# Turning the loops of a q and k projection, and sending a row of 1/rms through DRAM

## The reference

```python
h = rmsnorm(x, g_mix[l])
proj = h @ w_in[l]
qa = split_heads(proj[..., 0:MOBA_WIDTH], MOBA_HEADS)
ka = split_heads(proj[..., MOBA_WIDTH:2 * MOBA_WIDTH], MOBA_HEADS)
va = split_heads(proj[..., 2 * MOBA_WIDTH:o1], MOBA_HEADS)
qb = split_heads(proj[..., o1:o1 + SB_WIDTH], SB_HEADS)
kbh = split_heads(proj[..., o1 + SB_WIDTH:o1 + 2 * SB_WIDTH], SB_HEADS)
...
x = x + cross_attention(rmsnorm(x, g_cross[l]), rmsnorm(mem, g_mem[l]), w_xq[l], w_xkv[l], w_xo[l])
```

## Time and profile before

| | us |
|---|---|
| median of 3 runs | 451.23 |
| lowest, highest | 449.95, 452.59 |
| span of the profiled execution | 449.3 |
| PE busy in it | 438.3 (98%) |
| PEld busy | 400.4 (89%) |
| DVE busy | 271.3 (60%) |
| ACT busy | 213.4 (47%) |
| POOL busy | 25.1 (6%) |

### The profile page before, as it was taken

The page is one execution under the profiler, slowest core; times in us unless marked ns, Lnnn a source line. Parts: engine busy times, 40 slices in busy tenths (PEclk is TensorE's granted clock), DMA queues, the critical chain, the costliest instruction groups (busy, mean ns, idle before and its releaser), DMA issues.

```text
span 449.3 us, 6925 instructions
## 1 busy us (share of the span) xinstructions
PE 438.3 (98%) x2884; PEld 400.4 (89%) x2884; DVE 271.3 (60%) x340; ACT 213.4 (47%) x268; POOL 25.1 (6%) x39
## 2 busy tenths in 40 slices
PE   6999999999999999999999999999999999999993
PEld 6999988989998999988998889999999999999982
DVE  4769556866666534886567867655555555555525
ACT  5753338755545471382527654444444444444413
POOL 0079000000000000000020000000000000000001
PEclk9899999999999999999999999999999999999999
DMA  7998554333322235455443335555555555556002
GB/s 228 415 420 342 188 187 171 112 103 128 136 104 95 94 137 179 171 206 202 144 182 140 116 119 188 188 188 187 188 187 188 189 187 187 187 187 233 0 0 93
DMA packets 12970, 77.46 MB, mean 172 GB/s; under 512 B 1552, under 2 KB 2064, under 8 KB 4496
## 3 DMA queue, kind: packets, MB, share of 16 engines
q1 hardware_dynamic: 12800, 77.08, 46.9%
q10 hardware_dynamic: 144, 0.02, 0.0%
HBM read 76.04 MB, written 1.05 MB: 172 GB/s over the span
## 4 chain that ended last, share of the span: by engine, by line
PE 95%; DVE 1%; DMA 1%; ACT 1%; SPq 0%; issue 0%; POOLq 0%; POOL 0%; DVEq 0%; ACTq 0%
PE bank L856 41%; PE bank L875 33%; PE bank L971 11%; PE bank L1007 2%; DMA xT_raw<-in_xT_dram 1%; PE bank L1053 1%; PE bank L1008 1%; PE bank L929 1%; PE bank L1073 1%; PE bank L934 1%; PE bank L928 1%; PE bank L889 1%; DVE res L808 1%; PE bank L989 1%; PE bank L940 1%; DVE xs L814 0%
## 5 line engine op out<-in xcount | busy, mean ns | idle before, releaser
L554 DVE TENSOR_TENSOR w_lo<-raw,w_hi 128x2048 fp32r<-128x2048 f32 (+3 forms) x76 | 155.4, 2069 | 43.0 <-ACT w_hi L363 41.6
L363 ACT ACTIVATE w_hi<-raw 128x2048 fp32r<-128x2048 f32 x65 | 122.3, 1909 | 36.0 <-PE bank L856 19.4
L856 PE MATMUL bank<-hT_hi,w_hi 128*128 128x256 f32 x416 | 119.4, 287 | 2.9 <-DVE w_lo L554 2.4
L856 PE MATMUL bank<-hT_lo,w_hi 128*128 128x256 f32 x416 | 118.8, 286 | 0.0
L856 PE MATMUL bank<-hT_hi,w_lo 128*128 128x256 f32 x416 | 118.8, 286 | 0.0
L856 PEld LDWEIGHTS bank<-hT_hi,w_hi 128*128 128x128 f32 x416 | 81.0, 195 | 4.2 <-DVE hT_lo L576 2.6
L856 PEld LDWEIGHTS bank<-hT_lo,w_hi 128*128 128x128 f32 x416 | 81.0, 195 | 0.6
L856 PEld LDWEIGHTS bank<-hT_hi,w_lo 128*128 128x128 f32 x416 | 81.0, 195 | 0.0
L510 ACT ACTIVATE relu<-bank 128x512 f32<-128x512 f32 x16 | 9.6, 598 | 95.7 <-PE bank L856 95.7
L777 DVE TENSOR_TENSOR relu<-relu 128x512 f32<-128x512 f32 x16 | 11.1, 693 | 61.6 <-ACT relu L510 61.6
L875 PE MATMUL bank<-w_hi,aT_hi 128*128 128x512 f32 x144 | 46.0, 392 | 0.0
(11 more groups left out here) (156 smaller groups left out, 610.8 us busy)
## 6 DMA issues: line engine op xcount, KB each, us to landing
raw<-in_weights_dram SPq DMA_DIRECT2D x65, 1024.0 KB, 4.8
raw<-in_weights_dram SPq DMA_DIRECT2D x7, 256.0 KB, 6.3
raw<-in_weights_dram SPq DMA_DIRECT2D x2, 512.0 KB, 7.8
res<-in_x_dram SPq DMA_DIRECT2D x2, 512.0 KB, 11.9
mem_tok<-in_mem_dram SPq DMA_DIRECT2D x1, 1024.0 KB, 9.6
memT_raw<-in_memT_dram SPq DMA_DIRECT2D x1, 1024.0 KB, 8.3
out_dram<-xs SPq DMA_DIRECT2D x2, 512.0 KB, 2.6
xT_raw<-in_xT_dram SPq DMA_DIRECT2D x3, 256.0 KB, 5.5
```

The lines of the kernel that those rows point to most:

```text
L363: copy(w_hi[:, slot, :], raw[:, rslot, :], ACT.Copy).then_inc(w_hi_ready, 1)
L554: return nc.vector.tensor_tensor(dst, whole, high.bitcast(fp32), sub)
L856: last = mm(outs[m], w, v[:, k0 + k, :], start=first and n == 0, stop=k == nk - 1 and n == 2, skip_group_check=bool(kt_wait))
```

## The change

The first eight chunks are laid out anew: chunk k now holds the k-th 128 channels of all 2048 q and k columns. PE goes through k outermost; for each k it runs 16 column blocks m, three matmuls each, into all eight banks, which all stay open until k = 7. Chunks 0 to 2 come in pieces of whole column blocks: 2, 4 and 10 blocks for chunk 0, 8 and 8 for chunks 1 and 2. `xT` comes in eight transfers, one ahead of each k. The row of 1/rms goes to a scratch in DRAM in two transfers of 128 values, and comes back in two transfers that repeat it on all partitions, in SP's queue behind load 7 (for x) and load 14 (for the memory tokens). DVE takes all eight banks out one behind the other.

```diff
-    cols = [("w_in", 0, 8, base + 256 * j, 256) for base in (0, qkv) for j in range(4)]
+    cols = [("w_in", k, 1, (0, qkv), 1024) for k in range(8)]
...
-    X_PIECES = [(0, 1), (1, 2), (2, 4), (4, 6), (6, 8)]
-    PIECES = [(0, *p) for p in X_PIECES] + [(1, k, k + 2) for k in range(0, 8, 2)] + [(2, 0, 4), (2, 4, 8)]
+    QK = 16
+    PIECES = [(0, 0, 2), (0, 2, 6), (0, 6, 16), (1, 0, 8), (1, 8, 16), (2, 0, 8), (2, 8, 16)]
...
+            def row(j, n, ready, dst):
+                sp.wait_ge(rstd_ready, ready)
+                for t in range(TOK):
+                    sp.dma_start(rstd_dram[j, t * P:(t + 1) * P].rearrange("(p a) -> p a", a=1), rstd[:, n, t:t + 1])\
+                        .then_inc(rstd_out[j], 16)
+                sp.wait_ge(rstd_out[j], 32)
+                sp.dma_start(dst[:, 0, :], rstd_dram[j:j + 1, :].to_broadcast([P, SEQ])).then_inc(row_ready[j], 16)
+                sp.dma_start(dst[:, 1, :], rstd_dram[j:j + 1, :].to_broadcast([P, SEQ])).then_inc(row_ready[j], 16)
...
+                if c == 7:
+                    row(0, X, 1, rstd_row)
+                if c == 14:
+                    row(1, MEM, 2, mem_row)
...
-            dve.wait_ge(ident_ready, 1)
-            diagonal(X, 1)
-            split(4)
-            spread(rstd_row, X_ROW_BANK, 1)
-
-            dve.wait_ge(row_ready, 1)
+            split(8)
+            split(9)
+            dve.wait_ge(row_ready[0], 32)
             for c in range(8):
-                dve.wait_ge(w_used, c + 1)
+                dve.wait_ge(*((qk_done, c + 1) if c < 7 else (w_used, KT)))
                 nc.vector.scalar_tensor_tensor(flat(qkT[:, 2 * c:2 * c + 2, :]), bank[c][:, :],
                                                DH ** -0.5 if c % 4 < 2 else 1.0, flat(rstd_row[:, :, :]),
                                                ALU.mult, ALU.mult).then_inc(qk_evac, 1)
-                split(c + 5)
+            split(10)
+            split(11)
+            split(12)
...
-            for c in range(8):
-                if c == X_ROW_BANK:
-                    pe.wait_ge(row_ready, 1)
-                weights_T(c, hT_hi, hT_lo, 0, KT, halves(c), c + 1 if c > 2 else None,
-                          pieces_of(c) if c <= 2 else None,
-                          (lambda: spread_rstd(X_ROW_BANK, 1)) if c == 3 else None)
+            for k in range(KT):
+                pe.wait_ge(lo_done[X], k + 1)
+                if k > 2:
+                    pe.wait_ge(w_lo_ready, k + 1)
+                for m in range(QK):
+                    for i, (c, m0, m1) in enumerate(PIECES):
+                        if (c, m0) == (k, m):
+                            pe.wait_ge(*((w_lo_ready, c + 1) if m1 == QK else (piece_lo, piece_no(i))))
+                    wh, wl = w_hi[:, k % RING, m * P:m * P + P], w_lo[:, k % RAW, m * P:m * P + P]
+                    for n, (w, v) in enumerate(((wh, hT_hi), (wh, hT_lo), (wl, hT_hi))):
+                        last = mm(halves(m // 2)[m % 2], w, v[:, k, :], start=k == 0 and m % 2 == 0 and n == 0,
+                                  stop=k == KT - 1 and n == 2, skip_group_check=True)
+                    if k == KT - 1 and m % 2 and m + 1 < QK:
+                        last.then_inc(qk_done, 1)
+                last.then_inc(w_used, 1)
```

More of the change, by code:

```diff
@@ L244, in load_piece @@
             def load_piece(i):
[L245 to L257, removed]
+                c, m0, m1 = PIECES[i]
+                cols = slice(m0 * P, m1 * P)
+                sp.dma_start(raw[:, c, cols], weights[c, :, cols]).then_inc(raw_in[c] if m1 == QK else piece_in[i], 16)
+            def row(j, n, ready, dst):
[7 more added lines that the diff above has]
+            for k in range(KT):
+                sp.dma_start(xT_raw[:, k, :], xT[:, k, :]).then_inc(xT_in[k], 16)
+                for i, (c, _, _) in enumerate(PIECES):
+                    if c == k:
+                        load_piece(i)
+                if 3 <= k < RAW:
+                    load(k, k)
+                if k == 3:
+                    for t in range(TOK):
+                        sp.dma_start(res[:, t, :], x[0, t * P:(t + 1) * P, :]).then_inc(x_in[t], 16)
+            for c in range(RAW, LOOP0):
                 load(c, c % RAW, c - RAW + 1 if c >= RAW else None)
+                if c == 7:
+                    row(0, X, 1, rstd_row)
+                if c == 14:
+                    row(1, MEM, 2, mem_row)
                 if c == 8:
@@ L378, in split_piece @@
             def split_piece(i):
-                c, k0, k1 = PIECES[i]
-                cols = slice(k0 * 256, k1 * 256)
-                act.wait_ge(raw_in[c] if k1 == KT else piece_in[i], 16)
+                c, m0, m1 = PIECES[i]
+                cols = slice(m0 * P, m1 * P)
+                act.wait_ge(raw_in[c] if m1 == QK else piece_in[i], 16)
                 copy(w_hi[:, c, cols], raw[:, c, cols], ACT.Copy)\
-                    .then_inc(w_hi_ready if k1 == KT else piece_hi, 1)
+                    .then_inc(w_hi_ready if m1 == QK else piece_hi, 1)
             act.wait_ge(gains_in, 16)
[L386 to L396, removed]
+            for k in range(KT):
+                act.wait_ge(xT_in[k], 16)
+                high_in(X, k, hT_hi, xT_raw, G_MIX)
+                for i, (c, _, _) in enumerate(PIECES):
+                    if c == k:
+                        split_piece(i)
+                if k >= 3:
+                    split(k)
+                if k == 4:
+                    act.wait_ge(x_in[0], 16)
+                    copy(xs[:, 0, :], res[:, 0, :], ACT.Square, accum_out=stat[:, X, 0:1]).then_inc(sumsq_act, 1)
+            for c in range(8, 12):
                 split(c)
@@ L586, in diagonal @@
[L586 to L598, removed]
+                    .then_inc(w_lo_ready if m1 == QK else piece_lo, 1)
@@ L611, in _ @@
-            dve.wait_ge(ident_ready, 1)
-            diagonal(X, 1)
-            split(4)
-            spread(rstd_row, X_ROW_BANK, 1)
-            dve.wait_ge(row_ready, 1)
+            for k in range(KT):
+                low_in(X, k, hT_hi, hT_lo, xT_raw, G_MIX)
+                for i, (c, _, _) in enumerate(PIECES):
+                    if c == k:
+                        split_piece(i)
+                if k >= 3:
+                    split(k)
+                if k == 4:
+                    dve.wait_ge(x_in[1], 16)
+                    sum_squares(xs[:, 1, :], res[:, 1, :], X, 1).then_inc(sumsq_dve, 1)
@@ L1122, with columns @@
     chunks, _ = weight_chunks(width, xw, inputs["x"].shape[2], ff)
-    weights = np.stack([inputs[w][0, k0 * P:(k0 + nk) * P, c0:c0 + nc_].reshape(nk, P, nc_).transpose(1, 0, 2)
-                        .reshape(P, nk * nc_) for w, k0, nk, c0, nc_ in chunks])
+    def columns(c0, n):
+        return np.concatenate([np.arange(c, c + n) for c in (c0 if isinstance(c0, tuple) else (c0,))])
+    weights = np.stack([inputs[w][0, k0 * P:(k0 + nk) * P][:, columns(c0, n)].reshape(nk, P, -1).transpose(1, 0, 2)
+                        .reshape(P, -1) for w, k0, nk, c0, n in chunks])
     gains = np.concatenate([inputs[g][0].reshape(-1, P).T for g in ("g_mix", "g_cross", "g_mem", "g_mlp")], axis=1)
```

47 lines of the change are left out of this document (10 added, 37 removed).

## The result

The changed kernel takes 461.23 us (median of 4, 460.49 to 462.4) against 450.71 for the kernel before (449.95 to 452.59). The estimated ratio is 1.0225, 95% interval 1.0199 to 1.0252 (the two medians alone give 1.0233). It is 10.5 us slower; 0.5 us faster was forecast. The span of its profiled execution is 458.4 us, 9.1 more than before.

The account below looks back on a forecast made before the run. PE's stream of matmuls (98% busy) was taken as the bound, with 5.2 us lost at the start; +0.4 for the start and -0.9 for the spreads gave -0.5, so 450.7 us, range 447.0 to 452.6.

Parts of the forecast that it names:

- The start: First projection: PE idle until 11.5 for the 1280-column third piece, clock low up to 14.1; +0.4 us.
- the third piece lands early: Rival at the start: ACT takes the piece at 7.3, PE resumes at 10.0, clock kept; 448.0 us, chance 0.28.
- its extreme version: Start, by the skill's 2 us fixed and 436 GB/s: piece there at 5.5, 446.6 us; chance within 0.28.
- The loops turned: First projection: still 384 matmuls at 0.12 us, 46 us, with no PE starving after the start.
- eight banks in turn: First projection: PE changes banks every 6 matmuls; between -0.5 and +0.5 us for 64 changes, taken as 0.
- Banks taken out at the end: End of the first projection: DVE starts with the last k and ends 0.7 us after PE; cost 0.
- PE's two spreads: PE's two spreads of 1/rms leave the chain: -0.44 - 0.43 = -0.9 us.
- The row through DRAM: 1/rms round trips in SP's queue: x's row there at 37, wanted at 51; loads 8 and 15 in time; cost 0.
- 17 us for the whole trip: Length of the round trip in SP's queue given as the point from which the slower case decides.
- SP's round trip: Slower rival: each leg takes 16.8 us, load 8 goes 16 us too late; 467 us, chance 0.03 with bank changes.
- the bank changes: Slower case in the first projection: changing banks costs time, up to +0.5 us; chance 0.03 with the round trip.
- past 95: Late loads: load 15 held back 6 us or so near 68, PE at chunk 15 only past 95 us; cost 0.

Follow-up runs that it names:

- e10: Kernel before with its start alone changed: input in transfers of 128, 384 and 512 KiB, chunk 0 cut likewise; 454.07 us, ratio 1.0062.
- e6: Changed kernel with the two transfers into rstd_row reading 128 different 1 KB rows of xT, not one DRAM row 128 times; one execution, 453.99 us.
- e4: Changed kernel with turned loops alone: x's row set to 1, not moved, memory tokens' row made by PE as before; 448.86 us, ratio 0.9945.
- e3: Changed kernel with the memory tokens' row made by PE and DVE as before, x's row still through DRAM; 457.64 us, ratio 1.0138.
- e5: Changed kernel with four broadcasts of x's row instead of two; one execution, 464.14 us.
- e8: Kernel before with only the memory tokens' row sent through DRAM in SP's queue behind load 14; 455.67 us, ratio 1.0090.
- e9: Changed kernel with both rows on POOL's queue (448.85 us), then also chunk 0 in four pieces; 449.76 us, ratio 0.9966 to the kernel before.
- e11: Changed kernel with the four stores to DRAM reading one 512-byte row of constants from one partition; one execution, 448.24 us.
- e12: Changed kernel, complete, with 1/rms transposed on DVE so each store moves 4 rows of 128 bytes; 448.82 us, ratio 0.9944.
- e1: Changed kernel with x's row moved back in SP's queue, behind the load of the transposed memory tokens; 454.05 us, ratio 1.0045.
- e2: Changed kernel with DVE taking out the eight banks ahead of split 9, not behind it; 459.58 us, ratio 1.0186.

## Why the prediction was wrong, step by step

*The start* was mis-sized: +0.4 forecast, 2.4 us gained by the first v matmul, 0.44 of them the spread. The third piece was taken up at 7.22, not 8.8, and PE resumed at 10.08 with the clock kept: that is the rival "the third piece lands early" (7.3 and 10.0 there; the 5.5 of its extreme version did not come). My step used the byte rates of the trace of before; between 4 and 6 us they were 87 GB/s there and 360 in the changed kernel. Why is open: e10 gave 232. That the clock stayed is a matter of the execution: in e6, whose program is the same there, it fell, and the first v matmul came at 56.35, near the 56.7 that I forecast.

*The loops turned, eight banks in turn*: right. 0.12 us a matmul, no starving (e4). *Banks taken out at the end*: right where nothing holds DVE's splits (e4), wrong in the changed kernel, by way of the row (3 below).

*PE's two spreads*: both are out of the chain, -0.9 as forecast; no run takes them alone.

*The row through DRAM, "cost 0"*: this is the step that failed. It cost 8.8 us for x's row and 3.9 for the memory tokens' (e3, e4), since it held SP's queue and with it the loads 8 and 15. The step was wrong in four places.

1. Its sizes. I took 2.6 us for the store from a store of 512 KB; 128 pieces of 4 bytes took 7.35. I took 2.6 for a broadcast; it lands after 6.5 and puts off load 8 by 1.8 us each, issue included (e5). And 1/rms was ready at 31.7, not 29.8: POOL's second operation took 2.64 us, while DVE made a `w_lo` beside it, and 0.72 in the kernel before. Load 8 was issued at 39.9, not 34.
2. I gave load 8 the median landing of 4.8. Behind the broadcasts it took 9.6, and load 9 stands behind 1 MB of memory tokens.
3. The point from which it decides. I asked when PE wants chunk 8, and came to "17 us for the whole trip". What PE wants first is two banks taken out, and in DVE's program that stands behind splits 8 and 9. I had read that order, and put the banks' start at the last k as if nothing stood ahead. The trip held SP for 8.2 us, half of my limit, and cost 9 (5.9 of idle and 3.1 of low clock). My rival "SP's round trip" named the place, at 0.03 together with the bank changes, and with the wrong point.
4. The same for load 15: I compared it with PE at chunk 15, "past 95". DVE's split 15 stands ahead of `mo_pT`, which PE wants at 89.3 in the kernel before and at 95.2 in the changed one, while it comes to chunk 15 in the kernel before at 111.0 (e3, e8). And load 15 was not held for 6 us but for 12, from 73.9, when chunk 9 was used, to 85.6; the memory tokens' 1/rms alone was ready only at 76.4.

And of a wait I counted only its length. A third of the first wait's price is the low clock after it, 3.1 us. I had weighed the rule of the Trainium skill on throttling ("TensorE: Matmul & The Clock Gate", section "HAM oscillation") at the start alone. There PE was idle 0.96 and 1.31 us in the changed kernel, and the clock stayed; with 1.40 us in e6 and 1.18 in e9 it fell.

The Trainium skill, "DMA: Bandwidth & Descriptors", warns twice: by its "Specifications", transfers in pieces under 512 bytes need a read-modify-write, and by its section "Anatomy of one DMA — SWDGE (gpsimd) path", which is about transfers issued by POOL (my estimate for the third piece had used it for SP's), the last write's receipt can take surprisingly long when the target is HBM. The first agrees with e11 and e12 in kind (7.35 us for pieces of 4 bytes, 2.2 for 128, 1.4 for 512); no run separates the size of a piece from their number. The second does not explain it here, since e11 wrote to the same DRAM in 1.4, from SP's queue.

## What to carry to other kernels

When a wait is put into a DMA queue, go through everything behind it, and for each load through the program of the engine that consumes it: the deadline is set by what stands behind that load's use there, not by when PE wants the load itself. Turn per-partition scalars into rows before they are stored, and issue a round trip from a queue that carries nothing urgent, if the trip itself is in time there (in e9 it was not, by 0.7 us). Count a wait of PE with the clock that it may cost. When a gain fails to come, find the first instruction that is late: from the first `mo_pT` matmul to the end the kernel takes 360.0 us, within 0.1, in the eleven of these fourteen traces where the clock was kept there, so what is above that (e1, e2, e8) is the clock.

## What the hardware showed that I had not expected

- Two broadcasts of one 1 KB row of DRAM to 128 partitions landed after 5.5 and 7.5 us, the engines 97% busy for 68 GB/s between them; the same sizes from 128 rows of another tensor landed within 2.3 to 3.0 us, 93% busy for 187 GB/s (e6).
- Two stores of 128 x 4 bytes took 7.35 us on an idle queue, from the first issue to the end of the wait; of 4 x 128 bytes 2.2, of 1 x 512 bytes 1.4.
- After idle stretches of about 3 us the clock fell in some executions (2.96 us in e8, 3.56 in e1) and not in others (3.18 in the changed kernel, 3.31 in e6, 3.44 in e5), so one wait has two prices. The fall cost 1.4 us in e8 and 2.6 in e1.
- At the very start the starts of the matmuls tell more than PEclk: in e1 it reads 1.00 from 4 to 10 us while the matmuls start 0.21 us apart, and in the kernel before it reads 1.00 from 4 to 8 us while they start 0.23 apart up to 7.04.
